# Attention scores by row groups: 64 plain features of two heads in row halves, 32 rotated ones in four groups of 32 rows

## What is computed

```
q = (rms_norm(c_q, q_norm_g) @ w_uq).reshape(b, s, MLA_HEADS, QK_NOPE + QK_ROPE)
kv = (rms_norm(c_kv, kv_norm_g) @ w_ukv).reshape(b, s, MLA_HEADS, QK_NOPE + V_HEAD)
k = jnp.concatenate([k_nope, jnp.broadcast_to(k_rope[:, :, None, :], (b, s, MLA_HEADS, QK_ROPE))], -1)
q = rope_tail(rms_norm(q, q_head_g), cos, sin)
k = rope_tail(rms_norm(k, k_head_g), cos, sin)
...
sc = jnp.einsum('bqhd,bkhd->bhqk', q_blk, k).astype(jnp.float32) * scale
p = jax.nn.softmax(sc, axis=-1).astype(v.dtype)
return jnp.einsum('bhqk,bkhd->bqhd', p, v)
```

## Time and profile before

| | |
|---|---|
| runs | 2098.12, 2100.12, 2101.68 us, median 2100.12 |
| profiled execution | 2097.6 us, its span 2095.8 us |
| mean granted clock of TensorE | 0.962 |
| PE busy, PE weight load busy | 1871.4 us (89%), 989.3 us (47%) |
| DVE, ACT, POOL busy | 847.1, 523.3, 267.3 us |
| attention, pairs 0 to 7 | 1335.5 to 1542.9 us of the span |
| one pair of heads in steady state | 25.8 us |

### The profile page before, as it was taken

The page is one execution under the profiler, slowest core; times in us unless marked ns, Lnnn a source line. Parts: engine busy times, 40 slices in busy tenths (PEclk is TensorE's granted clock), DMA queues, the critical chain, the costliest instruction groups (busy, mean ns, idle before and its releaser), DMA issues.

```text
span 2095.8 us, 43853 instructions
## 1 busy us (share of the span) xinstructions
PE 1871.4 (89%) x19382; PEld 989.3 (47%) x19382; DVE 847.1 (40%) x1663; ACT 523.3 (25%) x1012; POOL 267.3 (13%) x296
## 2 busy tenths in 40 slices
PE   5899999999998958999999968899986799999888
PEld 2366766766667523333333325566643333333332
DVE  8655655755654241222222121577723222222211
ACT  2343443344343110111001012355521011101010
POOL 5223123113213110000000000111101000000000
PEclk8999999999999979999999998899998899999999
DMA  4001101101103469999999960300035999999997
GB/s 118 21 15 37 43 8 37 43 8 37 43 8 115 183 248 383 427 427 428 426 428 427 427 277 16 112 22 22 12 132 204 365 428 427 426 428 427 427 427 319
DMA packets 85414, 461.49 MB, mean 220 GB/s; under 512 B 16749, under 2 KB 49898, under 8 KB 60650
## 3 DMA queue, kind: packets, MB, share of 16 engines
q1 hardware_dynamic: 82922, 450.30, 52.8%
q0 software_dynamic: 2304, 8.39, 1.0%
HBM read 450.80 MB, written 7.86 MB: 219 GB/s over the span
## 4 chain that ended last, share of the span: by engine, by line
PE 61%; DMA 20%; DVE 7%; issue 5%; ACT 4%; DVEq 2%; SPq 0%; ACTq 0%; POOLq 0%; POOL 0%; another core or an unknown queue 0%
DMA arena<-in_moe_w_down 19%; PE banks L1620 13%; PE bank L564 8%; PE banks L1336 5%; PE bank L1620 5%; PE banks L847 5%; PE bank L1666 3%; ACT arena L2080 2%; PE banks L1666 2%; PE banks L951 2%; PE banks L1034 1%; PE banks L971 1%; PE banks L825 1%; PE banks L564 1%; PE banks L1600 1%
## 5 line engine op out<-in xcount | busy, mean ns | idle before, releaser
L1620 PE MATMUL banks<-arena 128*64 128x512 f32 x2560 | 568.9, 597 | 26.1 <-DMA arena<-in_moe_w_up 16.2
L1620 PEld LDWEIGHTS banks<-arena 128*64 128x64 f32 x2560 | 180.2, 137 | 378.4 <-issue 347.4
L1725 DVE TENSOR_TENSOR arena<-arena,bank 128x512 f32<-128x512 f32 x80 | 55.1, 688 | 319.9 <-PE bank L1666 319.9
L564 PE MATMUL bank<-arena 128*128 128x512 f32 x336 | 166.0, 616 | 1.0 <-DVE arena L1264 0.7
L1182 POOL TENSOR_TENSOR arena<-arena 128x512 f32<-128x512 f32 x80 | 101.1, 1290 | 415.7 <-DVE arena L1239 415.7
L847 PE MATMUL banks<-arena 64*64 64x64 f32 x5632 | 128.8, 223 | 15.4 <-issue 11.0
L1620 PE MATMUL bank<-arena 128*64 128x512 f32 x512 | 118.8, 615 | 24.9 <-DMA arena<-in_moe_w_down 24.9
L847 PEld LDWEIGHTS banks<-arena 64*64 64x64 f32 x5632 | 112.9, 136 | 54.3 <-issue 40.6
L1679 ACT ACTIVATE arena<-banks 128x512 f32<-128x512 f32 x32 | 19.1, 597 | 410.8 <-PE banks L1620 410.8
L1714 DVE SCALAR_TENSOR_TENSOR arena<-arena,banks 128x512 f32<-128x512 f32 x32 | 33.7, 1052 | 209.6 <-PE banks L1620 209.6
L1697 POOL DMA_INDIRECT arena<-out_dram,small x16 | 15.4, 965 | 783.1 <-DVE small L1703 783.1
(11 more groups left out here) (343 smaller groups left out, 2643.0 us busy)
## 6 DMA issues: line engine op xcount, KB each, us to landing
arena<-in_moe_w_gate SPq DMA_DIRECT2D x64, 2048.0 KB, 36.2
arena<-in_moe_w_up SPq DMA_DIRECT2D x64, 2048.0 KB, 38.2
arena<-in_moe_w_down SPq DMA_DIRECT2D x60, 2048.0 KB, 38.6
out_dram<-arena SPq DMA_DIRECT2D x12, 512.0 KB, 2.6
arena<-in_x SPq DMA_DIRECT2D x8, 512.0 KB, 5.2
arena<-in_rw_wr SPq DMA_DIRECT2D x8, 512.0 KB, 4.4
arena<-in_rw_wk SPq DMA_DIRECT2D x8, 512.0 KB, 5.8
arena<-in_rw_wv SPq DMA_DIRECT2D x8, 512.0 KB, 6.3
```

Of the source, the lines that this page charges most:

```text
L564: last = nc.tensor.matmul(b[:, :], w_sl[:, n, k, :], xmix[n][:, k, :], start=(k == 0), stop=(k == ND - 1))
L1620: last = nc.tensor.matmul(b[z * CAP:(z + 1) * CAP, :], st[:, k, :], ring[g % RING][:, k, z * 512:(z + 1) * 512], start=(c % 2 == 0 and k = ...
L1725: nc.vector.tensor_tensor(xs, xs, b[:, :], ALU.add).then_inc(free[COMB[j]], 1)
```

## The change

Queries and keys are laid out anew, so that the scores of both heads can use different rows of the array:

- The first transposed tile (128 rows) holds the plain 64 features of head 0 and of head 1. The second holds the 32 rotated features of head 0 and head 1, and the same two again: four groups of 32 rows.
- The score of (head, tile) becomes two matmuls into the same bank: one over 64 rows (L2056 of the new kernel; head 0 in rows 0 to 63, head 1 in 64 to 127), one over 32 rows that adds to it (L2066). Four of the latter, two heads by two tiles, lie in the four groups.
- The scores come by tile pairs z = 0, 1 for both heads instead of by heads, and the projections are cut at their halves: plain scores z=0, keys' first half, rotated scores z=0, keys' second half, plain scores z=1, queries' first half, rotated scores z=1, queries' second half. A rotated group waits for `nope_ready`, a semaphore that PE itself raises with the last plain matmul of its z.
- The job names, ACT's exponentials and DVE's maxima and divisions follow in the order z, then head. Head 0's transposes wait for 6 of the pair's 8 divided tiles, head 1's for all.
- ACT copies a query projection in two pieces (rotated part into a tile `q_rope`, plain part into the transposed layout). DVE scales a key part twice as wide (the rotated features stand twice) and copies the rotated queries into both places, a new instruction before `qk_ready`. Copies out of the transposes have 128 rows instead of 96; DVE's needs no gain.
- Two more small transfers bring the gains twice into their column, and a memset on POOL falls away.

```diff
-            names += [("S", u, 0, t) for t in range(NT)] + kv_ + [("S", u, 1, t) for t in range(NT)] + q_
+            names += [("S", u, h, t) for t in (0, 1) for h in range(2)] + kv_ + [("S", u, h, t) for t in (2, 3) for h in range(2)] + q_
...
-            for h in range(2):
-                b = open_job(pe, jobs, (kind, u, h))
-                for t in range(NT):
-                    last = nc.tensor.transpose(b[0:QK, t * P:(t + 1) * P], tok[:, 2 * t + h, :], ident[:, :])
-                last.then_inc(full[jobs[(kind, u, h)][0]], 1)
+            b = open_job(pe, jobs, (kind, u, 0))
+            for t in range(NT):
+                last = nc.tensor.transpose(b[:, t * P:(t + 1) * P], tok[:, t, 0:P], ident[:, :])
+            last.then_inc(full[jobs[(kind, u, 0)][0]], 1)
+            b = open_job(pe, jobs, (kind, u, 1))
+            for t in range(NT):
+                last = nc.tensor.transpose(b[:, t * P:(t + 1) * P], tok[:, t, P:2 * P], ident[:, :])
+            last.then_inc(full[jobs[(kind, u, 1)][0]], 1)
...
-                nc.scalar.copy(q_tok[:, 4 * z:4 * z + 4, :].rearrange("p g c -> p (g c)"), b[:, 0:4 * QK]).then_inc(free[jobs[("q", u, z)][0]], 1)
...
+                nc.scalar.copy(q_rope[:, 4 * z:4 * z + 4, :], q[:, :, NOPE:])
+                nc.scalar.copy(nope_of(q_tok)[:, 2 * z:2 * z + 2], q[:, :, 0:NOPE].rearrange('p (t h) c -> p t h c', h=2)).then_inc(free[jobs[("q", u, z)][0]], 1)
...
-                nc.vector.tensor_tensor(k_tok[:, :, NOPE:].rearrange("p (t h) c -> p t h c", h=2)[:, :, h, :], k_rope,
...
+                nc.vector.tensor_tensor(rope_of(k_tok)[:, :, :, h, :], k_rope.unsqueeze(2).to_broadcast([P, NT, 2, ROPE]),
...
+            dve.drain()
+            nc.vector.tensor_copy(rope_of(q_tok).rearrange("p t y h c -> p t y (h c)"),
+                                  q_rope.rearrange("p (t h) c -> p t (h c)", h=2).unsqueeze(2).to_broadcast([P, NT, 2, 2 * ROPE]))
...
+                def scores_nope(z):
+                    for t in (2 * z, 2 * z + 1):
+                        for h in range(2):
+                            q = slice(h * NOPE, (h + 1) * NOPE)
+                            b = open_job(pe, aj, ("S", u, h, t))
+                            last = nc.tensor.matmul(b[:, :], qkT[0][0][q, t * P:(t + 1) * P], qkT[0][1][q, :], start=True, stop=False, skip_group_check=True)
+                    last.then_inc(nope_ready, 1)
+
+                def scores_rope(z):
+                    pe.wait_ge(nope_ready, 2 * u + z + 1)
+                    for y in range(2):
+                        for h in range(2):
+                            q = slice((2 * y + h) * ROPE, (2 * y + h + 1) * ROPE)
+                            t = 2 * z + y
+                            b = aj[("S", u, h, t)][0]
+                            nc.tensor.matmul(ps[b][:, :], qkT[1][0][q, t * P:(t + 1) * P], qkT[1][1][q, :], start=False, stop=True,
+                                             skip_group_check=True).then_inc(full[b], 1)
+
+                for z, kind in enumerate(("kv", "q")):
+                    scores_nope(z)
+                    if more:
+                        if z == 0:
+                            pe.wait_ge(ld_pair2, (u + 2) * 32)
+                        project_heads(pe, aj, kind, u, (0,))
+                    scores_rope(z)
+                    if more:
+                        project_heads(pe, aj, kind, u, (1,))
...
-                    for t in range(NT):
-                        b = open_job(pe, aj, ("S", u, h, t))
-                        nc.tensor.matmul(b[:, :], qkT[h][0][0:QK, t * P:(t + 1) * P], qkT[h][1][0:QK, :],
-                                         start=True, stop=True).then_inc(full[aj[("S", u, h, t)][0]], 1)
-                    if h == 0 and more:
-                        pe.wait_ge(ld_pair2, (u + 2) * 32)
-                        project_heads(pe, aj, "kv", u)
-                    if h == 1 and more:
-                        project_heads(pe, aj, "q", u)
-                for h in range(2):
-                    pe.wait_ge(prob_ready, NT * (2 * u + h + 1))
+                    pe.wait_ge(prob_ready, 2 * NT * u + 6 + 2 * h)
...
-                row_max(0)
-                normed(0)
+                row_max(0, 0)
+                row_max(1, 0)
+                normed(0, 0)
+                normed(1, 0)
                 if more:
                     keys_sum_dve(dve, u)
-                row_max(1)
+                row_max(0, 1)
+                row_max(1, 1)
                 if more:
                     keys_scale_dve(dve, aj, u)
-                normed(1)
+                normed(0, 1)
+                normed(1, 1)
```

More of the change, by code:

```diff
@@ L1827, in mla_in_pool @@
                 nc.gpsimd.memset(freq[:, n:n + 1], float(np.float32(THETA) ** np.float32(-2.0 * n / ROPE)))
-            pool.drain()
-            nc.gpsimd.memset(gain_cols[NOPE:QK, :], 1.0)
             pool.drain().then_inc(freq_ready, 1)
@@ L1903, in trunk, with project_heads @@
         SCALE = QK ** -0.5
-        def project_heads(pe, jobs, kind, u):
+        def project_heads(pe, jobs, kind, u, zs=(0, 1)):
             w, n0, n, width = (wq_sl, 0, NQ, 2 * QK) if kind == "q" else (wkv_sl, NQ, NKV, 2 * (NOPE + VH))
-            for z in range(2):
+            for z in zs:
                 b = open_job(pe, jobs, (kind, u, z))
@@ L2048, in attn_pe @@
-                for h in range(2):
-                    pe.wait_ge(prob_ready, NT * (2 * u + h + 1))
+                    for i in range(2):
+                        job_read(pe, aj, ("Tk", u - 1, i))
+                        job_read(pe, aj, ("Tq", u - 1, i))
+                def scores_nope(z):
[5 more added lines that the diff above has]
+                    last.then_inc(nope_ready, 1)
@@ L2071, in attn_act @@
                 more = u < NPAIR - 1
-                for h in range(2):
-                    if u > 0:
-                        act.wait_ge(full[aj[("PT", u - 1, h, NT - 1)][0]], aj[("PT", u - 1, h, NT - 1)][1])
-                    for t in range(NT):
-                        n = NT * h + t
-                        act.wait_ge(max_ready, 4 * u + 2 * h + t // 2 + 1)
-                        b = job_full(act, aj, ("S", u, h, t))
-                        nc.scalar.activation(prob[h][:, t, :], b[:, :], ACT.Exp, bias=nmx[:, n:n + 1],
-                                             scale=q_scale[u % 2][:, 2 * t + h:2 * t + h + 1], accum_out=lsum[:, n:n + 1])
-                        act.drain().then_inc(free[aj[("S", u, h, t)][0]], 1)
-                    if h == 0 and more:
+                for z in range(2):
+                    for h in range(2):
+                        if z == 0 and u > 0:
+                            act.wait_ge(full[aj[("PT", u - 1, h, NT - 1)][0]], aj[("PT", u - 1, h, NT - 1)][1])
+                        act.wait_ge(max_ready, 4 * u + 2 * z + h + 1)
+                        for t in (2 * z, 2 * z + 1):
+                            n = NT * h + t
+                            b = job_full(act, aj, ("S", u, h, t))
+                            nc.scalar.activation(prob[h][:, t, :], b[:, :], ACT.Exp, bias=nmx[:, n:n + 1],
+                                                 scale=q_scale[u % 2][:, 2 * t + h:2 * t + h + 1], accum_out=lsum[:, n:n + 1])
+                            act.drain().then_inc(free[aj[("S", u, h, t)][0]], 1)
+                    if z == 0 and more:
                         keys_act(act, aj, u, v_tok[(u + 1) % 2])
@@ L2105, in attn_dve @@
                 more = u < NPAIR - 1
-                def row_max(h):
-                    for z in range(2):
-                        for t in (2 * z, 2 * z + 1):
-                            b = job_full(dve, aj, ("S", u, h, t))
-                            nc.vector.tensor_reduce(mx[:, NT * h + t:NT * h + t + 1], b[:, :], AX, ALU.max)
-                        if h == 0 and z == 0 and u > 0:
-                            dve.wait_ge(qkrstd_ready, u)
-                        dve.drain()
-                        n = NT * h + 2 * z
-                        nc.vector.tensor_tensor(nmx[:, n:n + 2], mx[:, n:n + 2],
-                                                q_scale_neg[u % 2].rearrange("p (t h) -> p h t", h=2)[:, h, 2 * z:2 * z + 2],
-                                                ALU.mult).then_inc(max_ready, 1)
@@ L2120, in normed, with row_max @@
-                def normed(h):
-                    for z in range(2):
-                        n = NT * h + 2 * z
-                        job_read(dve, aj, ("S", u, h, 2 * z))
-                        job_read(dve, aj, ("S", u, h, 2 * z + 1))
-                        nc.vector.reciprocal(linv[:, n:n + 2], lsum[:, n:n + 2])
-                        dve.drain()
-                        for t in (2 * z, 2 * z + 1):
-                            nc.vector.tensor_scalar(prob[h][:, t, :], prob[h][:, t, :], linv[:, NT * h + t:NT * h + t + 1], None,
-                                                    ALU.mult).then_inc(prob_ready, 1)
+                def row_max(h, z):
```

(22 more changed lines are left out.)

31 lines of the change are left out of this document (17 added, 14 removed).

## The result

| kernel | median, us | runs | profiled execution, us | its span, us |
|---|---|---|---|---|
| before | 2099.12 (2094.35 to 2101.68) | 4 | 2097.60 | 2095.8 |
| changed | 2156.99 (2155.23 to 2158.25) | 4 | 2158.25 | 2156.1 |

The changed kernel is slower: the ratio is 1.0278, 95% interval 1.0257 to 1.0298. The forecast was 2153 within 2134 to 2182, with 0.92 for slower.

A forecast was written before the change was run, and what follows sets the result against it. PE's work was taken as the bound, DVE's chain right behind. Terms 38.5 (pairs 0 to 6), 1.9 (last), 0.7 (making pair 0) and 11.9 (clock) make 53.0 on 2097.6; with 2.5 from profiled to median, 2153 us, range 2134 to 2182.

The forecast's parts named there:

- four groups of 32 rows, with the change: Rotated scores on PE: four matmuls run in parallel in 0.86 us, plus 0.20 for changing the array's division.
- PE's own work: PE in one pair: 1.7 us saved on scores, 1.6 lost to division changes, so unchanged within 0.2 us.
- transposes start: Head 0's transposes on PE, waiting for its sixth divided tile: start at 19.4 us instead of 14.3.
- open wait ahead of them: PE idle ahead of head 0's transposes until DVE's divisions: 3.7 us in a pair.
- pair at full clock: One pair with the 2.4 GHz level kept: grows by 5.5 us to 31.3 us.
- the clock, pairs 0 to 6: Low clock level behind the new wait delays PE's transposes 1.7 us a pair, 11.9 us in seven pairs.
- last pair: Pair without projections between: value product 0.9 us later plus a later start, 1.9 us in all.
- 2.6 us and 2066: Estimate from the skill's tiling speedups alone: a pair's scores fall from 6.9 to 2.6 us, total 2066 us.
- The bank's wait: Fourth plain matmul of z=1 on PE waits for the third exponential to free its bank: 2.0 us, until 9.65.
- The clock stays: Rival: clock stays at 1.00 behind the 3.7 us wait, total 2141 us; chance 0.25 for 2134 to 2146.
- PE is the bound: Rival: DVE and ACT catch up in PE's shadow, so only the scores' work counts, 2086 us; chance 0.04 with gain.
- Rows in series: Rival: row parts run one after the other, 6.9 us more PE work a pair, 2180 to 2195; chance 0.05.

The follow-up runs named there:

- e3: The changed kernel with four useless matmuls filling PE's wait ahead of head 0's transposes: 2144.08 us.
- e2: The changed kernel with rotated scores right behind the plain ones and whole projections behind both: 2134.09 us.
- e9: The kernel before, 96-row scores kept, with the order of e7 for scores, maxima, exponentials, divisions, key scaling and query work: 2091.30 us.
- e1: The kernel before, 96-row scores kept, with the changed order by tile pairs z but whole projections: 2110.29 us.
- e4: The changed kernel with the scores' jobs, and so their banks, numbered by head inside each z: 2150.89 us.
- e7: The changed kernel with rotated scores right behind plain, key scaling behind head 0's last divisions, DVE's query work behind head 1's copies: 2105.76 us.

## Why the prediction was right

Point by point, by its own steps, times from pair 1's first score:

| step | forecast | measured |
|---|---|---|
| four groups of 32 rows, with the change | 0.86 + 0.20 | 1.07 (1381.45 to 1382.52) |
| four plain scores z=0, with the change | 1.9 | 1.92 |
| first maximum of z=0, of z=1 | 4.9, 13.9 | 5.0, 13.9 |
| fourth plain score of z=1 starts | 9.65 | 9.58 |
| PE's own work in a pair, more than before | 0.2 at most | 1.0 |
| PE done with the queries' second half | 15.7 | 16.07 |
| transposes start | 19.4 | 19.9 (19.56 in pair 4) |
| open wait ahead of them | 3.7 | 3.50 to 3.85 |
| new DVE copy | 0.48 | 0.43 |
| pair at full clock | 31.3 | 32.04 (e3, pair 4) |
| pairs as run, by the signs named | 31 to 33 | 32.04 (pair 4), the others 33.4 to 36.6 |
| the clock, pairs 0 to 6 | 11.9 | 11.9 (e3) |
| last pair | +1.9 | +0.1 |
| making pair 0 | 0.7 | 0.8 |

**The mechanism held.** Row halves and the four groups ran in parallel, the gain on PE went into changes of the division, and the late maxima set the pair. e3 shows the clock's term by itself, and the ladder above how the rest is shared: 20.6 us for the two parts kept apart, 12.4 for the clock that is left then, 12.4 for the split itself, 9.8 for the order by z.

The Trainium skill ("TensorE: Matmul & The Clock Gate", Part 3, Measured speedup vs the span model) gives 3.07 times for four row tiles. The measurement decides: 1.07 us with one change, 0.87 without it, against four times 0.86, so four times within what the rows resolve. Its "TensorEngine Tiling", Key Properties, says that a change of tiling mode drains TensorE. The trace agrees as far as it shows a cost, 0.2 us a change. By that page's Theoretical Speedup the kernel should have gained. The prediction's 2.6 us and 2066 don't follow from the factors, though: eight matmuls of 0.86 at half and eight at a quarter are the 5.15 us of its own sum. Its PSUM Bottleneck section fits DVE's 19.02 us in the changed pair, which did not shrink; what decided is when the banks came full (e2, e9).

**Terms that were mis-sized.** By e3, pairs 0 to 6 grew by 226.9 - 183.63 = 43.27 with the clock kept up behind the wait, where 183.63 is before's 1519.16 - 1335.53, then by 11.9 for the clock, and the last pair by 0.1: 55.3. The forecast had 38.5, 11.9 and 1.9. That the clock's 11.9 came out to the digit is in part luck: the forecast was 1.7 in each of seven pairs, and between the changed kernel and e3 they are 2.2, 2.4, 1.4, 2.5, 0.0, 1.7 and 1.7.

- *The pair at full clock:* 0.7 short, 5 us in all. The transposes come 0.2 later. That is a slip in the prediction's sum: the terms of its key scaling, 0.69 and twice 0.41, are 1.51 us, but it counts 1.25 (16.85 to 18.1), and measured are 1.55 (1394.80 to 1396.35). The 0.29 that a step of it waits to issue is pair 1's alone. And the start of the next pair waits 0.99 us instead of 0.54, for DVE's second copy of the queries (L1961) rather than ACT's first. The prediction charged this wait, for all four copies, to the last pair only; every pair has it. e1 has 1.04 at the same place with the old layout, so it comes with the order by z, which needs both heads' queries at once.
- *The last pair:* +0.1 instead of +1.9. The prediction let head 1's transposes wait until 17.0; they run on from head 0's, which start at 14.5 instead of 15.0. How much that gives hangs on the clock behind PE's 8.23 us of idle ahead of them, which the changed kernel and e3 both have. The first two rows are the changed kernel from 1.1 us behind the transposes' start, the last three e3 from the same place, columns as the earlier trace rows:

```profile
1595.50:1597.50 2.00, 2.00 (x13) 2.00 (x12) 1.52 (x3) 0.84 (x2) 0.00 (x0) 0.59 0.01 4
1597.50:1599.50 2.00, 2.00 (x20) 1.83 (x20) 1.42 (x3) 1.39 (x3) 0.00 (x0) 1.00 0.00 0
```
```profile
1580.00:1582.00 2.00, 2.00 (x12) 2.00 (x11) 1.52 (x3) 0.84 (x2) 0.00 (x0) 0.50 0.01 4
1582.00:1584.00 2.00, 2.00 (x11) 2.00 (x10) 0.69 (x1) 0.88 (x2) 0.00 (x0) 0.50 0.00 0
1584.00:1588.00 4.00, 4.00 (x24) 2.12 (x24) 1.38 (x2) 0.62 (x2) 0.00 (x0) 0.94 0.00 0
```

  In e3 the low level holds 2.5 to 3 us longer, and its last pair is 25.85, 1.5 above before: near the 1.9. So 1.4 of the 1.8 missed are how long the low level lasted in one execution.
- *The bank's wait:* forecast as 2.0 us, from 7.6 to 9.65, and named as a sign. The idle is 0.76, since the third plain score runs in that time, alone, without its neighbour in the other row half. The end was as forecast, 10.6 instead of 10.5. e4 shows that this pairing was worth more than the idle: 6.5 us of the stage, 0.9 a pair.
- *PE's own work:* forecast as unchanged within 0.2 us. Up to the end of the query projection it is 16.07 - 0.76 = 15.31 us now and was 14.30. The lone third score makes most of it: three plain scores of z=1, here in pair 2, take as long as the four of z=0 (1.99).

```profile
1419.29 1.98 PE L2056 MATMUL banks<-arena 64*128 64x512 f32 x6
```

  It cost nothing here, since the fourth score waits for its bank until 9.58 anyway. PE's end at 16.07 instead of 15.7 lies in the shadow of DVE's chain and makes the open wait 3.5 us instead of 3.7.

**The rivals.** "The clock stays" (2141) would have been right in pair 4 and is what e3 builds: 2144. "PE is the bound" was to decide if DVE's chain behind the second rotated group took under 2 us: it took 1397.53 - 1391.55 = 6.0. "Rows in series" is excluded by the 1.07.

**What stays open.** Why pair 4 kept the 2.4 GHz level behind 3.50 us of idle, when its neighbours lost it behind 3.50 as well, no run settles. e7's DVE work (wider key part 0.26 us, the copy 0.43) was not tried with ACT or POOL doing it, nor an order that completes a first bank sooner at the price of more changes, so whether the split could be brought level with e9 isn't known.

## What to carry to other kernels

Packing matmuls into row groups shortens only the matmuls, and each change of the array's division takes back 0.2 us; ask first when the readers of the results get their first full bank, since maxima, exponentials and divisions keep their length and now start later. If a split result is completed by a second matmul, put that one right behind the first, and put other work behind both. Look for a wait inside a group of matmuls that run beside each other: removing one on DVE's queue, by moving one call, was worth 14 us of the stage, while the 1.7 us that the row groups save in a pair, before the changes are paid, are 12 at best.

## What the runs showed of the hardware

- Four float32 matmuls of 32 rows and 512 columns in four row groups took 1.07 us with a change of the array's division. Less the 0.2 that a change takes, that is 0.87, as long as one of 96 rows. I had expected that with a doubt.
- Three plain scores, two of them in the two row halves and one alone, took 1.98 us, as long as four in two pairs (1.99).
- A wait of 0.78 us between two matmuls that otherwise run in the two column halves costs 1.8 us.
- Idle time alone doesn't tell the clock, nor how long it stays low (above, behind 8.23 us). The granted clock stayed at 1.00 behind 0.86 (e1), 1.41 (e7) and, once, 3.50 us; it fell to 0.50 behind 2.36 (e2), although it stayed at 1.00 behind 2.61 in the kernel before.
